# A prefetched expert block in the room of a smaller descriptor ring: one core, one layer step with 32 experts

## The chip, the cores and the metric

The kernel runs on one core of one Trainium2 chip. The metric is the device time of one execution in microseconds (us). Three executions of the kernel before took 1171.94, 1173.74 and 1175.29 us; the median is 1173.74 us. All data are 32-bit floats in HBM, and all weights are read once.

## What is computed

One layer of a diffusion backbone for 128 context tokens and 128 latent tokens, model width 1024. Cut to what matters here:

```
mod = silu(c) @ w_ada + b_ada                      # six vectors of 1024 for each token group
h   = rmsnorm(x) * g_mix * (1 + scale) + shift
z   = h @ w_in                                     # pool 512 | q | k | v 512 each | gates 2 x 1024
a   = pool_mixer(z.pool, w_pool) @ w_pa
o   = attention(q, k, v, cache_k, cache_v, rpb) @ w_pb
x   = x + gate_m * ((sigmoid(ga) * a + sigmoid(gb) * o) @ w_out)
h2  = rmsnorm(x) * g_ffn * (1 + scale_f) + shift_f
p   = softmax over the top 4 of 32 of (h2 @ w_router + b_router)
for e in range(32):                                # each expert reads 8 MB of w_up and 4 MB of w_down
    u = h2 @ w_up[e] + b_up[e]
    y = ((clip(u.up) + 1) * glu(u.gate)) @ w_down[e] + b_down[e]
    acc += p[:, e] * y
out = rmsnorm(x + gate_f * acc) * g_final
```

## The kernel before

**Stages.** The prologue, up to about 204 us, computes everything up to the merged branches: modulation, input projection, attention, pooling, branch projections. Then come the output projection (TensorE line L1475), the norm and the router. From 250 us on, the experts are worked through in 16 pairs. The tokens of a pair are gathered into two groups of 64 rows, so that two experts fill the 128 output rows of the matmuls. A pair has eight up blocks and four down blocks. A block is one DMA of 2,048 KB: for up, one k-block of 128 rows of both experts (or two k-blocks of one expert); for down, the same amount. The experts thus read 192 blocks.

**Order of the pairs.** TensorE does the up blocks of pair Q, then the down blocks of pair Q-1, then gathers the rows of pair Q+1. The first pair's up blocks (`up_first`) are followed at once by the second pair's (`up_second`), both on line L1555. After these, up blocks are on line L1615 and down blocks on L1630. The last down blocks are on L1650.

**Buffers.** `ring` is 16 slots of 8 KB a partition. The prologue's weights use single slots, the experts use pairs of slots, so that eight blocks fit. SyncE (SP) issues all weights in one fixed order. The function `put(n, at, ...)` waits until the semaphore `moe_free` has counted `at + 1` and then issues ring block n. Eight counts come from the prologue, the router stage and the output projection, as they give their slots free; after that TensorE adds one for each ring block that it has finished. So ring block n is issued when ring block n-8 is finished. One further block, the first pair's k-block 7, goes to `spare`, a place in the 13,056-column scratch tensor `arena`, and adds nothing to `moe_free`; SP issues it once the residual is done (`x2_ready`). That makes nine blocks which can be under way before TensorE has finished its first one.

**The prologue's order.** `MIX` lists the prologue's weight chunks in SP's order. The last ten are chunks of the input projection, two of `w_pa`, two of `w_pb` and four of `w_out`. Each waits on `pro_used` or `O_done` until its slot is free. GpSimd (POOL) issues the small loads on its own queue: `w_pool`, eight pieces of the relative position bias `rpb`, `cache_k`, `cache_v`, `g_ffn`, `w_router`, `b_router`. Then it waits for `bias_copied`, masks the bias in eight steps (L476, L479) and raises `bias_ready`. VectorE waits for that at L911, and the splits of the gate weights into two parts (L893, L896) that TensorE needs next (L1292 to L1294) stand behind it.

```
# POOL
part_load(kc, A_cache_k[0, 0].rearrange("h l d -> l h d"), L["kc"])
...
part_load(brt[:, :], A_b_router.to_broadcast([P, E]), L["brt"])
pool.wait_ge(bias_copied, 1)
```

Of the kernel before, what the change touches and what calls it, by code (L numbers as in the profile page):

```python
# [13 lines left out]
P = 128  # L14
# [28 lines left out]
PC = UPC + DNC  # L43
BC = BODY * PC
LAPS = BC // RING
FIRST_UP = UPC - 1
NC = PAIRS * PC - 1
LOOPS = (PAIRS - 4) // BODY
VEC = 44

# [22 lines left out]
def layer_kernel(nc, A_x_prompt, A_x_sample, A_cache_k, A_cache_v, A_c, A_c_ctx, A_w_ada, A_b_ada, A_g_mix,  # L73
# [13 lines left out]
    with ExitStack() as ctx:  # L87
# [15 lines left out]
        selbuf = sb("selbuf", [96, 2, CAP], BF16)  # L103
        ident = sb("ident", [P, P])
        iota = sb("iota", [P, CAP])
        iota_i = sb("iota_i", [P, CAP], I32)
        tab = sb("tab", [P, PAIRS + 1, 8])
        cur = sb("cur", [P, 8])
        small = sb("small", [P, 256])
        flags = sb("flags", [P, 4], I32)  # L110
        mhalf = sb("mhalf", [P, 1])
        pick = sb("pick", [P, 4])
# [81 lines left out]
        Af = in_slot(13, 0, 2, D)  # L194
        shf = in_slot(15, 0, 2, D)

        vecs = sb("vecs", [VEC, P])
        cT = sb("cT", [P, VEC])
        gffn = in_slot(9, 0, D)
        cs = in_slot(9, 1024, KB, 32)  # L200
        wpool = in_slot(9, 1280, 4, P)
# [1 line left out]
        cnt = region(6720, 4, PW)  # L203
        wrt = sb("wrt", [P, KB, E])
        brt = sb("brt", [P, E])
        selrow = sb("selrow", [P, 2, P])
        tri = sb("tri", [P, P])
        ones = sb("ones", [P, P])
        rt = sb("rt", [P, 2, 8, E])

        Am = small[:, 0:16].rearrange("p (g k) -> p g k", g=2)
# [39 lines left out]
        scat_done, acc_done, woT_done, woT_ready = sem("scat_done"), sem("acc_done"), sem("woT_done"), sem("woT_ready")  # L251
        hT_done, hTe_ready, y_ready = sem("hT_done"), sem("hTe_ready"), sem("y_ready")
        hT_split, unit_ready, unit_used = sem("hT_split"), sem("unit_ready"), sem("unit_used")
        yT_split, oT_top_ready, w_top_ready = sem("yT_split"), sem("oT_top_ready"), sem("w_top_ready")
        cur_ready, glu_ready = sem("cur_ready"), sem("glu_ready")
        fin_ss, fin_lo, fin_hi, last_scat, stored = (sem("fin_ss"), sem("fin_lo"), sem("fin_hi"), sem("last_scat"),
# [36 lines left out]
        @block.sync  # L293
        def _(sp):
            def mixing_chunk(c):
                s = ring[:, mix_slot[c], :]
                kind, m, k = MIX[c]
                if kind == "first":
                    return (s.rearrange("p (k s n) -> p k s n", k=2, s=2), w_first_v[:, 2 * k:2 * k + 2, :, m, :])
                if kind == "ada":  # L300
                    return s, w_ada_v[:, k, m * SLOT:(m + 1) * SLOT]
                if kind == "in":
                    return (s.rearrange("p (k n) -> p k n", k=4),
                            w_in_v[:, 4 * k:4 * k + 4, m * HALF:(m + 1) * HALF])
                w = {"pa": w_pa_v, "pb": w_pb_v, "out": w_out_v}[kind]
                return s.rearrange("p (k n) -> p k n", k=2), w[:, 2 * k:2 * k + 2, :]

            for row, src in ((0, A_c_ctx), (8, A_c[0]), (16, A_g_mix[0])):
                sp.dma_start(vecs[row:row + 8, :], src.rearrange("(k p) -> k p", p=P)).then_inc(L["vec"], 16)
            sp.dma_start(vecs[24:28, :], A_pool_scale[0].rearrange("(k p) -> k p", p=P)).then_inc(L["vec"], 16)  # L310
            sp.dma_start(vecs[28:44, :], A_b_ada[0][0:2 * D].rearrange("(k p) -> k p", p=P)).then_inc(L["vec"], 16)
            sp.dma_start(x[:, 0, :], A_x_prompt[0]).then_inc(L["x0"], 16)
            sp.dma_start(x[:, 1, :], A_x_sample[0]).then_inc(L["x1"], 16)
            for c in range(len(MIX)):
                if mix_before[c] is not None:
                    sp.wait_ge(pro_used, mix_before[c] + 1)
                elif mix_slot[c] >= RING0:
                    sp.wait_ge(O_done, 1)
                dst, src = mixing_chunk(c)
                if MIX[c][0] == "first":  # L320
                    for j in range(2):
                        sp.dma_start(dst[:, j], src[:, j]).then_inc(pro_loaded[mix_slot[c]], 16)
                else:
                    sp.dma_start(dst, src).then_inc(pro_loaded[mix_slot[c]], 16)

            def stream(r):

                def put(n, at, src, dst=None):
                    sp.wait_ge(moe_free, at + 1)
                    sp.dma_start(pair_slot(n) if dst is None else dst, src).then_inc(moe_loaded[n % RING], 16)  # L330

                def rows(e, c):
                    return w_up_v[e, :, c // 2, :] if c < UPC else w_down_v[e, :, (c - UPC) // 2, :]

                def halves(n):
                    return pair_slot(n).rearrange("p (a n) -> p a n", a=2)

                N = r * NC
                for kk in range(FIRST_UP):
                    if kk == FIRST_UP - 1:  # L340
                        if r == 0:
                            sp.wait_ge(x2_ready, 4)
                        else:
                            sp.wait_ge(y_ready, 2 * (1 + r * PAIRS))
                        sp.dma_start(spare, up_rows(0, KB - 1)).then_inc(spare_loaded, 16)
                    put(N + kk, N + kk, up_rows(0, kk), halves(N + kk))

                n0 = N + FIRST_UP
                for kk in range(KB):
                    put(n0 + kk, n0 + kk, up_rows(2, kk), halves(n0 + kk))  # L350
                for c in range(DNC):
                    put(n0 + UPC + c, n0 + UPC + c, rows(c % 2, UPC + c))

                with sp.Fori(0, LOOPS) as i:
                    N0 = N + FIRST_UP + PC
                    n0 = sp.snap(i * BC + N0)
                    e0 = sp.snap(i * (2 * BODY) + 2)
                    for h in range(BODY):
                        for c in range(PC):
                            m = h * PC + c  # L360
                            e = e0 + (2 * h + c % 2 + (2 if c < UPC else 0))
                            put(N0 + m, n0 + m, rows(e, c))

                n0 = N + FIRST_UP + PC + LOOPS * BC
                for c in range(PC):
                    put(n0 + c, n0 + c, rows(E - (4 if c < UPC else 6) + c % 2, c))
                n0 += PC
                for kk in range(KB):
                    put(n0 + kk, n0 + kk, up_rows(E - 2, kk), halves(n0 + kk))
                n0 += UPC  # L370
                for c in range(DNC):
                    put(n0 + c, n0 + c, down_rows(E - 4, 2 * c, 2 * c + 2), halves(n0 + c))
                n0 += DNC
                for c in range(DNC - 1):
                    put(n0 + c, n0 + c, down_rows(E - 2, 2 * c, 2 * c + 2), halves(n0 + c))
                dst = halves(n0 + 3)
                sp.wait_ge(moe_free, n0 + 4)
                sp.dma_start(dst[:, :, 0:D], down_rows(E - 2, 6, 7)).then_inc(tail_loaded, 16)
                sp.dma_start(dst[:, :, D:2 * D], down_rows(E - 2, 7, 8)).then_inc(moe_loaded[(n0 + 3) % RING], 16)

            def up_rows(e, kk):
                return A_w_up[0][e:e + 2].rearrange("e (c p j) n -> p c j e n", p=P, j=2)[:, kk // 2, kk % 2]

            def down_rows(e, j0, j1):
                v = A_w_down[0][e:e + 2].rearrange("e (c p j) n -> p c e j n", p=P, j=4)
                v = v[:, j0 // 4, :, j0 % 4:(j1 - 1) % 4 + 1]
                return v.rearrange("p e j n -> p e (j n)")

            stream(0)
            further_rounds(sp, read_flags(sp), stream)  # L390

            for t, y in enumerate((y_prompt, y_sample)):
                sp.wait_ge(fin_lo, t + 1)
                sp.wait_ge(fin_hi, t + 1)
                sp.dma_start(y[0], x[:, t, :]).then_inc(stored, 16)
            sp.wait_ge(stored, 32)
            sp.wait_ge(kv_stored, 32)
# [811 lines left out]
        def _(pe):  # L1209
# [19 lines left out]
            def keep_busy(n, bank):  # L1229

                for _ in range(n):
                    mm(ps[:, bank, 0:TOK], tri[:, :], selrow[:, :, :].rearrange("p a b -> p (a b)"), start=True, stop=True)

            def first_rows(hf, chunks):

# [323 lines left out]
            def up_first(R, chunk, second_half):  # L1559

                up_bias(R)
                for kk in range(KB):
                    if kk % 4 == 0:
                        pe.wait_ge(xg_ready, R * 2 + (kk // 4 + 1))
                    if kk == 2 and second_half is not None:
                        gather(R, 1, second_half)
                    if kk < FIRST_UP:
                        up_block(0, kk, both_experts(chunk(kk), 2 * FF)).then_inc(moe_free, 1)
                    else:
                        pe.wait_ge(spare_loaded, 16 * (R // PAIRS + 1))  # L1570
                        up_block(0, kk, [spare[:, a, :] for a in range(2)]).then_inc(first_used, 1)
# [189 lines left out]
```

## Time and profile before

| | |
|---|---|
| median of three executions | 1173.74 us (1171.94 to 1175.29) |
| profiled execution, first to last instruction | 1172.6 us |
| median less that span | 1.1 us |
| HBM read | 457.51 MB, 392 GB/s over the span |
| TensorE matmul busy | 1068.0 us (91%) |
| VectorE, ScalarE, POOL busy | 304.9, 141.2, 42.7 us |
| granted TensorE clock, mean | 0.982 |

The profile's times are us from the first instruction. A matmul of float32 operands shows as two records. A wait is named by the instruction that stood waiting and by what ended the wait; "SPq" is SyncE, whose instructions only issue DMAs. For the profiled execution no time apart from the span is given, so the span is what sums are made against.

### The profile page before, as it was taken

The page shows a single profiled execution, that of the slowest core. Times are in us where ns is not written, and L with a number is a line of the kernel's source. Part 1 is how long each engine was busy: PE and PEld are TensorE (multiplying, and loading weights), DVE is VectorE, ACT ScalarE, POOL GpSimd, SP SyncE. Part 2 cuts the span into 40 slices and gives each one's busy share as a digit, 9 for nine tenths or more (in the row PEclk, how much of TensorE's full clock was granted, in tenths as well). Part 3 has the DMA queues.
Part 4 walks back from the last instruction along what each step waited for, and adds up shares of the span by engine and source line. Part 5 has one row for each costly group of instructions (what it writes and reads, how often), then busy time and mean ns, then how long its engine had stood idle before and what let it go on. Part 6 is the DMA issues. An engine that isn't in the chain of part 4 may idle for free.

```text
span 1172.6 us, 13196 instructions
## 1 busy us (share of the span) xinstructions
PE 1068.0 (91%) x5399; PEld 505.0 (43%) x5399; DVE 304.9 (26%) x585; ACT 141.2 (12%) x275; POOL 42.7 (4%) x79
## 2 busy tenths in 40 slices
PE   7989999999999989898989897979898989797987
PEld 5755798454343424343434242424242424242422
DVE  3042767742212121212121212121212121212125
ACT  2013324111010101000001010101010101010111
POOL 3004000000000000000000000000000000000000
PEclk9999999999999999999999999999999999999999
DMA  9988464899999999999999999999999999999995
GB/s 333 407 325 259 169 258 139 339 421 422 429 418 429 428 426 429 429 428 429 428 429 428 429 429 428 428 428 429 428 429 429 428 429 429 428 429 422 421 421 215
DMA packets 51248, 459.64 MB, mean 392 GB/s; under 512 B 4444, under 2 KB 4504, under 8 KB 20648
## 3 DMA queue, kind: packets, MB, share of 16 engines
q1 hardware_dynamic: 49960, 455.12, 93.3%
q0 software_dynamic: 1024, 3.29, 1.1%
q10 hardware_dynamic: 224, 0.69, 0.2%
q8 instruction: 25, 0.41, 0.1%
q14 instruction: 15, 0.12, 0.0%
HBM read 457.51 MB, written 1.57 MB: 392 GB/s over the span
## 4 chain that ended last, share of the span: by engine, by line
PE 63%; DMA 31%; DVE 2%; issue 1%; SPq 1%; ACT 1%; POOL 0%; DVEq 0%; POOLq 0%; ACTq 0%
DMA ring<-in_w_down_dram 30%; PE ps L1615 17%; PE ps L1630 10%; PE ps L1555 6%; PE ps L1508 5%; PE ps L1519 5%; PE ps L1261 4%; PE ps L1475 2%; PE ps L1650 2%; PE ps L1277 1%; PE ps L1548 1%; PE ps L1535 1%; PE ps L1292 1%; PE ps L1294 1%; PE ps L1293 1%
## 5 line engine op out<-in xcount | busy, mean ns | idle before, releaser
L1615 PE MATMUL ps<-ring,arena 128*64 128x512 f32 x1664 | 364.5, 593 | 17.9 <-DMA ring<-in_w_up_dram 17.9
L1630 PE MATMUL ps<-ring,arena 128*64 128x512 f32 x896 | 209.1, 622 | 53.3 <-DMA ring<-in_w_down_dram 53.3
L1615 PEld LDWEIGHTS ps<-ring,arena 128*64 128x64 f32 x1664 | 121.0, 137 | 244.8 <-issue 242.5
L1630 PEld LDWEIGHTS ps<-ring,arena 128*64 128x64 f32 x896 | 72.5, 143 | 189.5 <-issue 170.5
L1115 DVE TENSOR_TENSOR arena<-ps,arena 128x512 f32<-128x512 f32 x64 | 44.2, 691 | 296.1 <-PE ps L1519 296.1
L1096 DVE TENSOR_SCALAR arena<-ps 128x512 f32<-128x512 f32 x32 | 20.6, 686 | 259.0 <-PE ps L1615 220.7
L1555 PE MATMUL ps<-ring,arena 128*64 128x512 f32 x368 | 80.8, 594 | 0.7 <-DVE arena L1098 0.7
L1508 PE MATMUL ps<-arena 128*128 128x128 f32 x512 | 63.6, 282 | 0.0
L1508 PEld LDWEIGHTS ps<-arena 128*128 128x128 f32 x512 | 61.7, 196 | 2.6 <-issue 2.4
L1519 PE MATMUL ps<-arena 128*128 128x512 f32 x128 | 57.8, 594 | 1.2 <-ACT arena L716 1.2
L1084 DVE TENSOR_SCALAR arena<-arena,cur 128x64 f32<-128x64 f32 x64 | 12.0, 249 | 162.7 <-PE ps L1527 160.2
L703 ACT ACTIVATE arena<-arena 128x512 f32<-128x512 f32 x32 | 19.5, 629 | 271.7 <-DVE arena L1096 271.7
L1555 PEld LDWEIGHTS ps<-ring,arena 128*64 128x64 f32 x368 | 26.2, 137 | 50.0 <-issue 48.4
L716 ACT ACTIVATE arena<-ps 128x512 f32<-128x512 f32 x30 | 16.3, 594 | 243.0 <-PE ps L1630 234.7
L1261 PE MATMUL ps<-ring 128*128 128x256 f32 x192 | 43.1, 384 | 0.0
L501 POOL COPY selbuf<-sel 96x128 bf16 (+1 forms) x16 | 11.2, 700 | 819.3 <-DVE arena L1098 811.1
L1261 PEld LDWEIGHTS ps<-ring 128*128 128x128 f32 x192 | 36.7, 193 | 7.1 <-issue 2.1
L1292 PE MATMUL ps<-parts 128*128 128x256 f32 x128 | 37.4, 292 | 1.9 <-DVE parts L896 1.9
L1294 PE MATMUL ps<-parts 128*128 128x256 f32 x128 | 36.9, 289 | 0.0
L1293 PE MATMUL ps<-parts 128*128 128x256 f32 x128 | 36.9, 288 | 0.0
L1106 DVE SCALAR_TENSOR_TENSOR arena<-arena 128x512 f32<-128x512 f32 x32 | 35.0, 1095 | 1.1
L1519 PEld LDWEIGHTS ps<-arena 128*128 128x128 f32 x128 | 23.1, 190 | 25.8 <-issue 23.8
(235 smaller groups left out, 802.4 us busy)
## 6 DMA issues: line engine op xcount, KB each, us to landing
ring<-in_w_up_dram SPq DMA_DIRECT2D x127, 2048.0 KB, 26.9
ring<-in_w_down_dram SPq DMA_DIRECT2D x63, 2048.0 KB, 23.2
ring<-in_w_in_dram SPq DMA_DIRECT2D x16, 1024.0 KB, 10.0
ring<-in_w_ada_dram SPq DMA_DIRECT2D x16, 1024.0 KB, 11.4
ring<-in_w_ada_dram SPq DMA_DIRECT2D x16, 512.0 KB, 11.7
ring<-in_w_out_dram SPq DMA_DIRECT2D x4, 1024.0 KB, 11.3
ring<-in_w_pa_dram SPq DMA_DIRECT2D x2, 1024.0 KB, 10.9
ring<-in_w_pb_dram SPq DMA_DIRECT2D x2, 1024.0 KB, 6.0
```

The costliest lines, as they stand in the source:

```text
L1106: V.scalar_tensor_tensor(out=gate[:, c].rearrange("q (j p) -> q j p", j=4), in0=hid[:, c].rearrange("q (p j) -> q j p", j=4), scalar=1.0, ...
L1115: V.tensor_tensor(acc[:, t, c], ps[:, SB + n, :], acc[:, t, c], ALU.add).then_inc(acc_done, 1)
L1261: ins = mm(ps[:, bank + b // 2, (b % 2) * TOK:(b % 2 + 1) * TOK], w[:, kk % 4, b * P:(b + 1) * P], hTm[:, kk, :], start=False, stop=(kk == ...
L1292: mm(out, w_top[:, n % 2, kk, :], hT_top[:, kk, :], start=(kk == 0), stop=False)
L1293: mm(out, w_top[:, n % 2, kk, :], hT_rest[:, kk, :], start=False, stop=False)
L1294: ins = mm(out, w_rest[:, n % 2, kk, :], hT_top[:, kk, :], start=False, stop=(kk == KB - 1))
L1475: ins = mm(ps[:, 2 * t + n, :], sgA[:, kk, t * P:(t + 1) * P], wo_[kk // 2][:, kk % 2, n * HALF:(n + 1) * HALF], start=(kk == 0), stop=(kk ...
L1508: ins = mm(ps[:, bank, (j % 4) * P:(j % 4 + 1) * P], h2[:, t, 2 * P * (j // 2) + j % 2:2 * P * (j // 2 + 1):2], oh[:, t, :], start=(t == 0 ...
L1519: mm(ps[:, SB + n, :], woT[:, t, :], yb[:, (n % 2) * HALF:(n % 2 + 1) * HALF], start=True, stop=True).then_inc(scat_done, 1)
L1555: ins = mm(ps[CAP * a:CAP * a + CAP, n, :], xgT[:, h, kk, CAP * a:CAP * a + CAP], w[a][:, n * HALF:(n + 1) * HALF], start=first, stop=(kk ...
L1615: ins = mm(ps[CAP * a:CAP * a + CAP, n, :], xgT[:, h, kk, CAP * a:CAP * a + CAP], w[a][:, n * HALF:(n + 1) * HALF], start=False, stop=(kk ...
L1630: ins = mm(ps[CAP * a:CAP * a + CAP, YB + n, :], hT[:, f, CAP * a:CAP * a + CAP], w[a][:, n * HALF:(n + 1) * HALF], start=(f == 0), stop=( ...
```

## The change

The descriptor ring of POOL's DMAs is set to 2,048 bytes a partition. `iota_i`, `cT`, `vecs` and `selrow` become places in `arena`, `small` is cut from 256 to 112 columns, and `tri` and `ones` become one tensor. The filler matmuls of `keep_busy` read `tri` and `ones` in place of `selrow`. A new tensor `early` of 4096 columns holds k-block 6 of the first pair. SP issues its load before the first chunk of `w_out`, with no wait. `FIRST_UP`, the number of the first pair's blocks that go through the ring, falls from 7 to 6, and the ring carries 190 blocks in place of 191. The load of `spare` comes behind all six. TensorE waits for `early_loaded` before k-block 6.

```diff
-FIRST_UP = UPC - 1
-NC = PAIRS * PC - 1
+FIRST_UP = UPC - 2
+NC = PAIRS * PC - 2
...
-        iota_i = sb("iota_i", [P, CAP], I32)
...
-        small = sb("small", [P, 256])
+        small = sb("small", [P, 112])
...
-        vecs = sb("vecs", [VEC, P])
-        cT = sb("cT", [P, VEC])
+        early = sb("early", [P, 2 * 2 * FF])
+        cT = region(11808, VEC)
+        vecs = arena[0:VEC, 11852:11852 + P]
+        iota_i = region(11984, CAP).bitcast(I32)
...
-        selrow = sb("selrow", [P, 2, P])
-        tri = sb("tri", [P, P])
-        ones = sb("ones", [P, P])
+        selrow = region(12800, 2, P)
+        masks = sb("masks", [P, 2, P])
+        tri, ones = masks[:, 0, :], masks[:, 1, :]
...
+            def load_early(r):
+
+                if r:
+                    sp.wait_ge(first_used, r)
+                sp.dma_start(early[:, :].rearrange("p (a n) -> p a n", a=2), up_rows(0, KB - 2)).then_inc(early_loaded, 16)
...
             for c in range(len(MIX)):
+                if c == AT["out", 0, 0]:
+                    load_early(0)
...
                 for kk in range(FIRST_UP):
-                    if kk == FIRST_UP - 1:
-                        if r == 0:
-                            sp.wait_ge(x2_ready, 4)
-                        else:
-                            sp.wait_ge(y_ready, 2 * (1 + r * PAIRS))
-                        sp.dma_start(spare, up_rows(0, KB - 1)).then_inc(spare_loaded, 16)
                     put(N + kk, N + kk, up_rows(0, kk), halves(N + kk))
+                if r == 0:
+                    sp.wait_ge(x2_ready, 4)
+                else:
+                    load_early(r)
+                    sp.wait_ge(y_ready, 2 * (1 + r * PAIRS))
+                sp.dma_start(spare, up_rows(0, KB - 1)).then_inc(spare_loaded, 16)
...
-                    mm(ps[:, bank, 0:TOK], tri[:, :], selrow[:, :, :].rearrange("p a b -> p (a b)"), start=True, stop=True)
+                    mm(ps[:, bank, 0:TOK], tri[:, :], masks[:, :, :].rearrange("p a b -> p (a b)"), start=True, stop=True)
...
                     if kk < FIRST_UP:
                         up_block(0, kk, both_experts(chunk(kk), 2 * FF)).then_inc(moe_free, 1)
+                    elif kk < KB - 1:
+                        pe.wait_ge(early_loaded, 16 * (R // PAIRS + 1))
+                        up_block(0, kk, both_experts(early[:, :], 2 * FF))
...
-    nc = _bacc.Bacc("TRN2", target_bir_lowering=False, num_devices=1)
+    nc = _bacc.Bacc("TRN2", target_bir_lowering=False, num_devices=1, dynamic_dma_scratch_size=2048)
```

## Rows read from the trace of the kernel before

**Rows 1.** The page, the span in 40 slices of 29.3 us.
```profile
GB/s 333 407 325 259 169 258 139 339 421 422 429 418 429 428 426 429 429 428 429 428 429 428 429 429 428 428 428 429 428 429 429 428 429 429 428 429 422 421 421 215
```

**Rows 2.** Waits on TensorE, 405 to 1137 us: total, times, longest.
```profile
PE ps L1630 <- DMA ring<-in_w_down_dram: 53.3, 24, 2.8
PE ps L1615 <- DMA ring<-in_w_up_dram: 17.9, 11, 2.0
```

**Rows 3.** Waits on TensorE, 250 to 405 us: the only one.
```profile
PE ps L1555 <- DVE arena L1098: 0.7, 1, 0.7
```

**Rows 4.** Chain that ended last, 340 to 411 us: start, length, what.
```profile
407.80 23.41 DMA ring<-in_w_down_dram
```

**Rows 5.** Windows: busy of each engine, clock, DMA share, GB/s.
```profile
166.00:168.00 2.00, 2.00 (x19) 2.00 (x18) 0.87 (x2) 0.00 (x0) 0.00 (x0) 1.00 0.00 0
...
350.00:352.00 2.00, 2.00 (x12) 0.42 (x7) 0.00 (x0) 0.00 (x0) 0.00 (x0) 1.00 0.82 279
...
411.00:1137.00 726.00, 651.85 (x3102) 261.72 (x3098) 128.87 (x242) 60.75 (x112) 9.11 (x12) 0.98 1.01 428
```

**Rows 6.** Timeline of SyncE: start, length, line, DMA, count.
```profile
157.74 0.89 SPq L324 DMA_DIRECT2D ring<-in_w_pb_dram  x2
170.62 6.27 SPq L324 DMA_DIRECT2D ring<-in_w_out_dram  x4
...
286.38 14.88 SPq L330 DMA_DIRECT2D ring<-in_w_down_dram  x4
...
348.92 8.29 SPq L330 DMA_DIRECT2D ring<-in_w_down_dram  x4
```

**Rows 7.** Waits on SyncE, 250 to 410 us.
```profile
SPq L330 <- PE ps L1615: 53.6, 6, 15.0
```

**Rows 8.** DMAs issued at 229.83, 286.38, 333.40, 348.92: us to landing.
```profile
ring<-in_w_up_dram SPq DMA_DIRECT2D x1, 2048.0 KB, 7.1
...
ring<-in_w_down_dram SPq DMA_DIRECT2D x1, 2048.0 KB, 11.4
...
ring<-in_w_up_dram SPq DMA_DIRECT2D x1, 2048.0 KB, 18.2
...
ring<-in_w_down_dram SPq DMA_DIRECT2D x1, 2048.0 KB, 7.7
```

**Rows 9.** Timeline of POOL, 86 to 111 us.
```profile
87.74 1.01 POOL L403 DMA_DIRECT2D ring<-in_w_pool_dram  x1 [75.61 <-DMA ring<-in_w_in_dram]
88.74 4.89 POOL L403 DMA_DIRECT2D ring<-in_rpb_dram  x8
...
94.52 0.89 POOL L403 DMA_DIRECT2D ring<-in_cache_v_dram  x1
...
96.84 0.56 POOL L403 DMA_DIRECT2D brt<-in_b_router_dram  x1
110.60 1.11 POOL L476 TENSOR_SCALAR_AFFINE_SELECT ring<-ring 64x384 f32<-64x384 f32 x1 [13.20 <-ACT ring L587]
```

**Rows 10.** The page's DMA issues on POOL's queue: median us to landing.
```profile
out_dram<-ring POOLq DMA_DIRECT2D x1, 256.0 KB, 3.2
...
ring<-in_w_pool_dram POOLq DMA_DIRECT2D x1, 256.0 KB, 7.6
...
ring<-in_rpb_dram POOLq DMA_DIRECT2D x8, 64.0 KB, 9.1
```

**Rows 11.** Waits on VectorE, 105 to 125, and on TensorE, 86 to 206.
```profile
DVE ring L911 <- POOLq L483: 4.1, 1, 4.1
...
PE ps L1292 <- DVE parts L896: 1.9, 1, 1.9
```

**Rows 12.** Window behind that wait of TensorE, columns as in rows 5.
```profile
120.00:124.00 4.00, 3.96 (x20) 3.96 (x21) 3.30 (x6) 0.00 (x0) 0.00 (x0) 0.57 0.00 0
```

**Rows 13.** Timeline of TensorE: bias flip and output projection.
```profile
107.44 1.95 PE L1355 MATMUL ps<-ring 128*128 128x512 f32 x4 [1.42 <-DVE arena L828]
...
204.65 22.56 PE L1475 MATMUL ps<-ring,arena 128*128 128x512 f32 x52 [0.41 <-PE ps L1439]
```

More of the change, by code:

```diff
@@ L253, in layer_kernel @@
         hT_split, unit_ready, unit_used = sem("hT_split"), sem("unit_ready"), sem("unit_used")
+        early_loaded = sem("early_loaded")
         yT_split, oT_top_ready, w_top_ready = sem("yT_split"), sem("oT_top_ready"), sem("w_top_ready")
@@ L313, in _, with up_rows @@
             sp.dma_start(x[:, 1, :], A_x_sample[0]).then_inc(L["x1"], 16)
+            def load_early(r):
+                if r:
+                    sp.wait_ge(first_used, r)
+                sp.dma_start(early[:, :].rearrange("p (a n) -> p a n", a=2), up_rows(0, KB - 2)).then_inc(early_loaded, 16)
+            def up_rows(e, kk):
+                return A_w_up[0][e:e + 2].rearrange("e (c p j) n -> p c j e n", p=P, j=2)[:, kk // 2, kk % 2]
             for c in range(len(MIX)):
+                if c == AT["out", 0, 0]:
+                    load_early(0)
                 if mix_before[c] is not None:
@@ L379, in stream @@
                 sp.dma_start(dst[:, :, D:2 * D], down_rows(E - 2, 7, 8)).then_inc(moe_loaded[(n0 + 3) % RING], 16)
-            def up_rows(e, kk):
-                return A_w_up[0][e:e + 2].rearrange("e (c p j) n -> p c j e n", p=P, j=2)[:, kk // 2, kk % 2]
             def down_rows(e, j0, j1):
```

## Prediction

> **What bounds the kernel now.** I read the rates of the page's slices first [rows 1]. From the ninth slice on, the weight stream runs at 418 to 429 GB/s but for the last slice; before that there are holes, down to 139 GB/s. So a load that is moved into a hole should take its time off the stream behind it. That holds only where the stream sets the pace, so the next view is the waits of TensorE by stage. Between 405 and 1137 us TensorE waits for weights again and again, 71.2 us in all [rows 2]. Between 250 and 405 us it waits for no weights at all, and for only 0.7 us of anything [rows 3]. The chain of work that ended last says the same: it enters the weight stream for good with the block issued at 407.80 us [rows 4]. Before that the chain lies on TensorE. The reader is to see two stages. Up to about 405 us TensorE is behind, and the stream must wait for it. After that the stream is behind, and the end of the program is the end of the stream plus a fixed tail.
>
> The pace of the stream is one block of 2,097,152 bytes at 428 GB/s [rows 5], which is 4.90 us. This is the most that one block loaded ahead can bring.
>
> **The early load itself.** It is one issue on SP and one block. SP has issued `w_pb` by 157.74 + 0.89 = 158.63 us and then waits until 170.62 us for a slot [rows 6]. The new issue needs no slot, so it goes out at about 158.7 us. The two pieces of `w_pb` (2 MB) are before it in the queue, and between 166 and 168 us nothing at all is moved [rows 5]. Its 4.90 us fit ahead of 170.62 us, so `w_out`, which TensorE needs at 204.65 us [rows 13], isn't delayed. Cost 0; if the hole were gone, `w_out` would land 4.9 us later, and with it the whole of the 34 us until then would have to be used up before that cost anything.
>
> **What follows for the stream.** Number the blocks in the order in which TensorE uses them: P0 to P7 are the first pair's up blocks, P8 to P15 the second pair's, P16 to P19 the first pair's down blocks, P20 to P27 the third pair's up blocks, P28 the next down block. Before, ring block n is P(n+1) for n of 7 and more, and it needs ring block n-8 finished, that is P(n-7). So P(j) needs P(j-8). After, ring block n is P(n+2) for n of 6 and more and needs P(n-6). Again P(j) needs P(j-8). With `early` and `spare` emptied once and not used again, the one block more of room exists only at the start. From P16 on, the earliest moment at which a block may be issued is the same as before, and it is set by TensorE.
>
> Now the slack. On an empty queue a block lands 7.1 us after its issue (up, issued at 229.83) [rows 8]. P16 is issued at 286.38 us [rows 6] and lands after 11.4 us [rows 8], so it stands about 11.4 - 7.7 = 3.7 us behind others. With the stream 4.9 us ahead that slack is gone, the queue runs dry for about 1.2 us, and 3.7 us of the lead are left. P28 is issued at 348.92 us [rows 6], after SP has waited 15.0 us for TensorE's L1615 [rows 7]. It lands after 7.7 us [rows 8], at 356.6 us. The block before it was issued at 333.40 and landed 18.2 us later, at 351.6 us [rows 8]; one block of streaming behind that is 356.5 us. So P28 found the queue just empty already in the kernel before. In the window from 350 to 352 us the rate falls to 279 GB/s [rows 5], a loss of 2 x (1 - 279/428) = 0.7 us. In the changed kernel the blocks before P28 land up to 3.7 us sooner, the queue waits for TensorE, and P28 starts at the same moment. The lead of 4.9 us has become idle time of the DMA engines before 350 us. Gain: 0 us by the landings, at most 0.7 us if all of that dip goes. I take 0.
>
> TensorE itself gets no earlier start: it has no wait for weights in that stage [rows 3], its eight blocks of the first pair are the same matmuls, and the filler matmuls read other data of the same shape. Those edits, the smaller `small` and the moved tables cost nothing: no instruction is added on VectorE, ScalarE or POOL. The wait for `early_loaded` is met 100 us before. The `spare` load keeps its place in time, as it waited for `x2_ready` behind the same six blocks.
>
> **The smaller descriptor ring.** This is the part that can cost. POOL issues 14 loads from 87.74 to 97.40 us (96.84 + 0.56) [rows 9]. The first lands only after 7.6 us, at 95.3 us, and the bias pieces after 9.1 us in the median [rows 10]. So by the time anything has landed nearly all are under way, and POOL was never held. The next work of POOL is the masking at 110.60 us [rows 9]: 13.2 us of room. Behind it stands VectorE's L911, which waited 4.1 us for it, and behind that the splits, for which TensorE waited 1.9 us [rows 11]. So whatever delays the masking past 110.60 us goes into the time one for one, because all up to 405 us hangs on TensorE.
>
> The loads aren't alike in pieces: `cache_k`, `cache_v` and `w_router` are 1024 contiguous runs each (128 partitions by 8), `w_pool` 512, each of the eight bias pieces 256, the other two 128 each. That is 5,888 runs, of which 4,608 (all up to `cache_v`, whose issue begins at 94.52 us) go out with nothing landed [rows 9]. The old ring thus took at least 4,608 runs, and one of an eighth of its bytes is sure to take 576 only. How much more it takes, and whether POOL stands still until a whole older load has landed, no row shows. From below: if room comes free as single runs are moved, POOL's last issue slips by less than the 13.2 us, cost 0. From above: `cache_k` must wait for about the fifth bias piece, issued at 88.74 + 4 x 4.89/8 = 91.2 us [rows 9], which lands 9.1 us later or some more, near 101 us; `cache_v` must wait for `cache_k`, and `w_router` for `cache_v`. A load of 256 KB takes 3.2 us on a quiet queue and 7.6 us beside the weights [rows 10]. The last issue then ends at 101 + 2 x 3.2 + 1.5 = 108.9 us to 101 + 2 x 7.6 + 1.5 = 117.7 us, where 1.5 us is the issue of the last two loads. Against 110.60 us this is 0 to 7.1 us. SyncE's loads are nearly done by then, so I lean to the quiet row, and take 1 us for the likeliest case, with 3 us as its upper end. The bias pieces must land before TensorE's L1355 at 107.44 us [rows 13]; the last can be issued near 97 us and lands near 106 us, so they still come in time.
>
> A longer idle of TensorE has a second price. After its 1.9 us of waiting the granted clock is 0.57 over 120 to 124 us, most of it at the lower of the two levels, 1.2 GHz [rows 12]. About 1.7 us are lost there already (4 us x 0.43). If the idle time grows to 5 us or more, I allow 1 us more.
>
> **The sum.** Span 1172.6 us; early load 0; lead of the stream 0 (bounds -0.7 and -4.9); POOL's ring +1 (bounds 0 and +8 with the clock): 1173.6 us of span. The median of the runs stands 1.1 us above the profiled span, so 1174.7 us.
>
> **Rivals.** (a) The lead is kept: the stream stays one block ahead to the end and the time falls by 4.9 us, to 1168.8 us. For it: the holes before the ninth slice [rows 1], and 71 us of waits for weights later [rows 2]. Against it: P28's landing 7.7 us after its issue and SP's wait of 15.0 us for TensorE. It would need TensorE to finish P20 at least 4.9 us earlier. (b) The ring stalls POOL and the masking slips by 4 to 8 us: 1178 to 1182 us. For it: the chain through L911 has no slack. Against it: 13.2 us of room and few weights in the queues after 100 us. It decides once POOL's last issue ends later than 114 us. The Trainium skill, "Debugging Trainium Hangs", section 4, Descriptor Overflow, speaks for this direction: it gives POOL's descriptors a finite room of 16 KiB a partition and names too many of them as a cause of hangs. (c) The early load gets in the way of others on the shared engines. It runs from about 165 to 170 us, where between 166 and 168 us nothing else is moved [rows 5], so I give it nothing of its own.
>
> **How the numbers follow.** A run of this kernel tells a change from none at about 0.3%, 3.5 us. No lead and a stall of 0 to 3 us: 0.65, time 1173 to 1177. Rival (b): 0.23. Rival (a): 0.08. The remaining 0.04 is for effects of placement I can't see, to either side. Faster by over 0.3%: 0.10; within: 0.65; slower: 0.25. The range must hold 8 in 10. It takes the likeliest case, half of (b) and the near side of (a): 1170.5 to 1180.0 us.
>
> **What would show it.** In the profile after, the early block is issued near 158.7 us. P16 is issued near 286.4 us and P28 near 348.9 us, both plus the delay of the masking, and both land 7 to 8 us after their issue; the DMA rate dips in some windows between 286 and 350 us where it did not before. TensorE's first wait for weights comes as long after its first up block as before. POOL's last load issue ends before 111 us, or the masking starts as much later as the whole program ends later. I'm wrong if P28 is issued, relative to TensorE's start on the experts at 250 us, earlier than before, or if the time falls by more than 3.5 us.

## The result

The changed kernel takes 1180.26 us in the median of four executions (1177.73 to 1181.25), the kernel before 1172.84 us over four (1171.5 to 1175.29). The ratio is 1.0058 with a 95% interval of 1.0046 to 1.0070: slower by 7 us. The forecast was 1174.7 us in a range of 1170.5 to 1180.0 us; the median lies 0.3 us above that range. The profiled execution took 1181.18 us for a span of 1179.4 us, 6.8 us more than the span of the kernel before.

The rates of the page's slices, beside [rows 1]. The stream is slower than before in the ninth to eleventh slice (391, 402 and 392 GB/s in place of 421, 422 and 429) and in the thirteenth (401 in place of 429):

```profile
GB/s 333 408 302 269 165 286 171 307 391 402 392 430 401 428 428 427 428 430 429 428 427 428 429 429 429 427 428 429 429 430 427 428 429 430 430 427 424 420 421 215
```

Timeline of POOL, columns as in [rows 9]:

```profile
89.44 1.01 POOL L413 DMA_DIRECT2D ring<-in_w_pool_dram  x1 [77.29 <-DMA ring<-in_w_in_dram]
90.44 3.07 POOL L413 DMA_DIRECT2D ring<-in_rpb_dram  x5
97.26 1.24 POOL L413 DMA_DIRECT2D ring<-in_rpb_dram  x2 [3.75 <-issue]
104.79 0.62 POOL L413 DMA_DIRECT2D ring<-in_rpb_dram  x1 [6.29 <-issue]
105.40 0.90 POOL L413 DMA_DIRECT2D ring<-in_cache_k_dram  x1
112.36 0.90 POOL L413 DMA_DIRECT2D ring<-in_cache_v_dram  x1 [6.06 <-issue]
113.25 0.56 POOL L413 DMA_DIRECT2D ring<-in_g_ffn_dram  x1
116.35 0.90 POOL L413 DMA_DIRECT2D wrt<-in_w_router_dram  x1 [2.54 <-issue]
117.24 0.56 POOL L413 DMA_DIRECT2D brt<-in_b_router_dram  x1
117.81 0.58 POOL L486 TENSOR_SCALAR_AFFINE_SELECT ring<-ring 64x384 f32<-64x384 f32 x1
```

POOL stands still four times, 3.75 + 6.29 + 6.06 + 2.54 = 18.6 us. The profile puts these waits down to "issue", as there is no semaphore of the program behind them. Each stop ends 0.3 to 0.4 us after a whole load has landed: `w_pool` at 96.95 us, the seventh bias piece at 104.40, `cache_k` at 112.02, `cache_v` at 116.04. The masking starts the moment the last load is out, at 117.81 us in place of 110.60. Who waits for it, on VectorE (105 to 135 us) and on TensorE (86 to 130 us), beside [rows 11]:

```profile
DVE ring L921 <- POOLq L493: 7.9, 1, 7.9
```

```profile
PE ps L1302 <- DVE parts L906: 5.3, 1, 5.3
...
PE ps L1365 <- DMA ring<-in_rpb_dram: 2.6, 1, 2.6
```

TensorE waits 5.3 us for the split weights in place of 1.9, and 2.6 us for the late bias piece. From here on the whole program is late by one amount: the expert stage's first up matmul starts at 256.85 us in place of 250.01.

SyncE's timeline, columns as in [rows 6]:

```profile
165.51 0.47 SPq L320 DMA_DIRECT2D early<-in_w_up_dram  x1
177.46 6.31 SPq L337 DMA_DIRECT2D ring<-in_w_out_dram  x4
...
293.21 14.88 SPq L343 DMA_DIRECT2D ring<-in_w_down_dram  x4
...
355.75 8.29 SPq L343 DMA_DIRECT2D ring<-in_w_down_dram  x4
```

P16 goes out at 293.21 and P28 at 355.75, both 6.83 us later than in [rows 6], neither a moment sooner against TensorE. What they took to land, each in a query of its own, beside [rows 8]:

```profile
ring<-in_w_down_dram SPq DMA_DIRECT2D x1, 2048.0 KB, 7.5
...
ring<-in_w_down_dram SPq DMA_DIRECT2D x1, 2048.0 KB, 7.6
```

P16 took 11.4 us before. Now both meet an empty queue. Two windows, columns as in [rows 5]:

```profile
286.00:296.00 10.00, 9.27 (x51) 4.61 (x48) 5.92 (x7) 3.03 (x4) 0.29 (x1) 1.00 0.90 340
...
411.00:1137.00 726.00, 655.23 (x3108) 265.02 (x3106) 130.00 (x248) 59.68 (x110) 9.12 (x12) 0.98 1.01 428
```

A first part of the lead is spent here: around 290 us the DMA engines are idle for a time (340 GB/s). The long stage behind runs at 428 GB/s as before.

The records of issue and landing show where the rest goes. Counted from the first up matmul of the experts, so that what happened in the prologue drops out (us, issue and landing):

| block | before | changed |
|---|---|---|
| P16 | 36.4, 47.7 | 36.4, 43.9 |
| P18 | 46.3, 57.5 | 46.3, 55.3 |
| P27 | 83.4, 101.6 | 83.4, 100.6 |
| P28 | 98.9, 106.6 | 98.9, 106.6 |
| P30 | 106.3, 117.4 | 106.3, 117.7 |
| end of the span | 922.6 | 922.5 |

Every issue from P16 to P30 is at the same place. The lead of the landings is 3.8 us at P16, 2.2 us at P18, 1.0 us at P27 and gone at P28. TensorE's first wait for weights begins 170.8 us after its first up block in both.

### The profile page after: what moved, and what is told of

It is laid out like the page before. It is cut to its first block, busy times and chain, and to the rows that moved or that the text cites. A ratio compares the mean times of both kernels' runs of the same rounds, so it can differ in the third digit from the quotient of the medians.

```text
span 1179.4 us, 13214 instructions
## 1 busy us (share of the span) xinstructions
PE 1072.1 (91%) x5399; PEld 508.9 (43%) x5399; DVE 305.4 (26%) x585; ACT 141.3 (12%) x275; POOL 42.2 (4%) x79
## 3 DMA queue, kind: packets, MB, share of 16 engines
q0 software_dynamic: 1024, 3.29, 1.0%
## 4 chain that ended last, share of the span: by engine, by line
PE 61%; DMA 31%; issue 3%; DVE 2%; POOL 1%; SPq 1%; ACT 1%; DVEq 0%; POOLq 0%; ACTq 0%
DMA ring<-in_w_down_dram 30%; PE ps L1628 17%; PE ps L1643 10%; PE ps L1565 6%; PE ps L1518 5%; PE ps L1529 5%; PE ps L1271 4%; PE ps L1485 2%; PE ps L1663 2%; PE ps L1558 1%; PE ps L1545 1%; PE ps L1302 1%; PE ps L1304 1%; PE ps L1303 1%; PE ps L1235 1%
## 5 line engine op out<-in xcount | busy, mean ns | idle before, releaser
L1565 PEld LDWEIGHTS ps<-ring,arena 128*64 128x64 f32 x352 | 25.0, 137 | 47.7 <-issue 46.1
```

What stands on the lines that cost most here:

```text
L1565: ins = mm(ps[CAP * a:CAP * a + CAP, n, :], xgT[:, h, kk, CAP * a:CAP * a + CAP], w[a][:, n * HALF:(n + 1) * HALF], start=first, stop=(kk ...
```

## The experiments

Each run was timed beside the kernel before; ratios are to that kernel and given with their 95% intervals. Changes are against the kernel named.

**The ring alone.** Against the kernel before:

```diff
-    nc = _bacc.Bacc("TRN2", target_bir_lowering=False, num_devices=1)
+    nc = _bacc.Bacc("TRN2", target_bir_lowering=False, num_devices=1, dynamic_dma_scratch_size=2048)
```

> The kernel before with the ring of 2,048 bytes and nothing else. Theory A (the whole loss is POOL standing still for room in the ring): POOL's last load is issued near 117.2 us in place of 96.8, the masking starts near 117.8 in place of 110.6, and the time is 6 to 7.5 us over the kernel before (ratio 1.005 to 1.006). Theory B (placement of the small tensors, or the early load in the way of others, makes the loss): within 1.5 us of the kernel before.

Measured: 1178.76 us, ratio 1.0049 (1.0037 to 1.0061). POOL's timeline:

```profile
101.76 0.62 POOL L403 DMA_DIRECT2D ring<-in_rpb_dram  x1 [6.20 <-issue]
...
109.73 0.90 POOL L403 DMA_DIRECT2D ring<-in_cache_v_dram  x1 [6.46 <-issue]
...
115.28 0.58 POOL L476 TENSOR_SCALAR_AFFINE_SELECT ring<-ring 64x384 f32<-64x384 f32 x1
```

The stops are at the same four places, and the time is 5.7 us over the kernel before by the ratio, just under the 6 to 7.5 us expected. The masking starts at 115.28 us and not near 117.8, but POOL began at 86.29 us in this execution: from the first load to the masking it is 29.0 us, in the changed kernel 28.4, before 22.9 [rows 9]. So one argument of the builder makes the slowdown, and no placement or early load is needed for it. The 1 us between this and the changed kernel is within the two intervals.

**The loads on another queue, with and without the early block.** Against the changed kernel, and the same against the kernel before:

```diff
 # POOL
-            pool.wait_ge(pro_loaded[mix_slot[c_after]], 16 * mix_held[c_after])
-            part_load(wpool, ...)          # and the 13 loads behind it
 # ScalarE, behind z_out(2)
+            act.wait_ge(pro_loaded[mix_slot[c_after]], 16 * mix_held[c_after])
+            act_load(wpool, ...)           # the same 14 loads in the same order
             act.wait_ge(pool_done, 1)
```

> The changed kernel, with POOL's 14 prologue loads issued by ScalarE, which makes no use of the small ring. Theory A with P(j) needs P(j-8): no stall, the early block is loaded, and the time is that of the kernel before to within 1 us, with P28 landing 7 to 8 us after its issue. Theory C (the lead is kept, the stall only hid it): 4.9 us under the kernel before, 1168 us. Theory B: still 5 us or more over the kernel before.

> Control: the kernel before, large ring, with the same 14 loads issued by ScalarE. Theory A: within 1 us of the kernel before and within 1 us of the run with the early block. Theory C: 4 to 5 us slower than the run with the early block.

Measured: 1172.73 us, ratio 0.9999 (0.9989 to 1.0009) with the early block, 1173.58 us, ratio 0.9999 (0.9990 to 1.0008) without. The loss is gone, and no gain is behind it. P16 again met an empty queue, landing 7.5 us after its issue, and P28 after 7.8 us. This settles it against the rival that the lead is kept. The first of the two has the moved tensors, the early load and the ring of 2,048 bytes of the changed kernel, so none of these shows a cost once POOL's 14 loads no longer go through the ring.

**A semaphore for each bias piece.** In the changed kernel the eighth piece went out at 104.79 us. The first had landed at 98.42 and the seventh at 104.40. All eight raise one semaphore. Against the changed kernel:

```diff
-                        part_load(dst, src, L["rpb"])
+                        part_load(dst, src, rpb_sems[4 * r + 2 * kr + par])
...
-            pe.wait_ge(L["rpb"], 16 * 8)
+            for s in rpb_sems:
+                pe.wait_ge(s, 16)
```

> The changed kernel with a semaphore of its own for each of the eight bias pieces. In the changed kernel the eighth piece was issued at 104.79, right after the seventh had landed, though the first had landed at 98.4. If POOL waits by the shared semaphore's count, the eighth now goes out near 98.8 us, cache_k near 102 or later, the masking starts 3 to 5 us sooner than 117.8 and the time falls by as much, to about 1176. If POOL waits for room in the order of issue whatever the semaphore, nothing changes: 1180.

Measured: 1176.66 us, ratio 1.0036 (1.0019 to 1.0053), 2.6 us better than the changed kernel by the ratios. But the two intervals overlap and the nine executions spread from 1175.33 to 1182.78 us, so the gain in time is likely and not shown; the trace shows what POOL does. Its timeline:

```profile
86.54 1.01 POOL L414 DMA_DIRECT2D ring<-in_w_pool_dram  x1 [74.41 <-DMA ring<-in_w_in_dram]
87.54 3.08 POOL L414 DMA_DIRECT2D ring<-in_rpb_dram  x5
94.65 1.99 POOL L414 DMA_DIRECT2D ring<-in_rpb_dram  x3 [4.03 <-issue]
100.11 0.90 POOL L414 DMA_DIRECT2D ring<-in_cache_k_dram  x1 [3.47 <-issue]
105.26 0.90 POOL L414 DMA_DIRECT2D ring<-in_cache_v_dram  x1 [4.25 <-issue]
...
111.02 0.90 POOL L414 DMA_DIRECT2D wrt<-in_w_router_dram  x1 [4.19 <-issue]
```

The eighth piece goes out with the other two, at 96.02 us, 0.3 us after the first had landed (95.71). `cache_k` goes 0.4 us after the landing of the fifth piece (99.75). From first load to masking it is now 25.9 us (112.48 - 86.54), 2.4 us less. So it matters whether the loads that POOL waits for share a semaphore. With one each it waits for the landing of single pieces; with one for all it waited for the seventh.

**A ring of 4,096 bytes.** Against the kernel before, as in the first run, with 4096.

> The kernel before with a ring of 4,096 bytes and nothing else. 
Measured: 1173.50 us, ratio 1.0002 (0.9993 to 1.0011). POOL's timeline:

```profile
88.82 4.91 POOL L403 DMA_DIRECT2D ring<-in_rpb_dram  x8
93.73 0.90 POOL L403 DMA_DIRECT2D ring<-in_cache_k_dram  x1
103.58 0.90 POOL L403 DMA_DIRECT2D ring<-in_cache_v_dram  x1 [8.95 <-issue]
...
105.92 0.56 POOL L403 DMA_DIRECT2D brt<-in_b_router_dram  x1
109.64 0.58 POOL L476 TENSOR_SCALAR_AFFINE_SELECT ring<-ring 64x384 f32<-64x384 f32 x1 [3.15 <-ACT ring L587]
```

One stop of 8.95 us, which ends 0.4 us after the eighth bias piece has landed (103.14 us). It costs nothing: the last load is out at 106.48 us, and the masking waits for ScalarE as before. Here a stall of POOL is free up to the point where ScalarE brings it its input.

**Less work on TensorE ahead of P8.** This is to see whether a free slot is all that the lead lacks. Both kernels have the loads on ScalarE. They leave out three quarters of the up product of k-blocks 1 to 3 of the first pair:

```diff
-            def up_block(h, kk, w, first=False):
-                for n in range(4):
+            def up_block(h, kk, w, first=False, groups=range(4)):
+                for n in groups:
...
-                        up_block(0, kk, both_experts(chunk(kk), 2 * FF)).then_inc(moe_free, 1)
+                        up_block(0, kk, both_experts(chunk(kk), 2 * FF),
+                                 groups=range(3, 4) if kk in (1, 2, 3) else range(4)).then_inc(moe_free, 1)
```

> The kernel before with the loads on ScalarE, and k-blocks 1 to 3 of the first pair multiply one of their four column groups in place of all four, so that part of the first pair's up product is left out. That takes 3 x 0.75 x 3.44 = 7.7 us from TensorE ahead of P8. Theory A (with the ring full the stream waits for TensorE up to P28, and just meets it there without the early block): the stream was running without a break already, so the time falls by at most 1 us, to 1172.5 to 1173.5. Rival (TensorE alone sets the pace up to P28): it falls by all of 7.7 us, to 1166.

> The changed kernel with the loads on ScalarE and the same matmuls of the first pair left out. Theory A: now the slots come free soon enough, the queue never runs dry, and the block loaded ahead is worth its 4 to 4.9 us: 4 us or more under the run without the early block. If the early block is worth nothing for another reason, the two are the same to within 1 us.

Measured: without the early block 1173.35 us, ratio 0.9999 (0.9990 to 1.0008); with it 1169.26 us, ratio 0.9961 (0.9947 to 0.9974). So 7.7 us less work on TensorE are worth nothing alone, and the early block is worth nothing alone, but both together are worth 4.1 us. From the first up matmul P16 is issued at 28.6 us in both, and P28 lands at 106.9 us without and at 101.7 us with the early block, 5.1 us sooner, and 4.9 us of it are left at the end of the span. Windows of the run with the early block, where the changed kernel with the loads on ScalarE and all its work had 370 and 419 GB/s:

```profile
280.00:300.00 20.00, 20.00 (x100) 8.62 (x97) 2.61 (x4) 1.68 (x3) 0.00 (x0) 1.00 1.02 428
300.00:345.00 45.00, 45.00 (x221) 17.99 (x219) 11.76 (x23) 4.87 (x9) 0.69 (x1) 1.00 1.01 428
```

**The same with all work done, first try.** TensorE's scatter of the rows of pair Q-1 is moved behind the slots that it held up. Against the changed kernel with the loads on ScalarE:

```diff
                         gather(Q + 1, b, GB + b)
-                    scatter(Q)
...
 # up and up_last
                 for kk in range(KB):
+                    if kk == 2:
+                        scatter(Q - 1)
                     if kk == 3:
                         turn_weights(Q - 1)
```

In the second pair the gather went from kk == 2 to 3, the hidden rows' transposes from 3 to 4 and the bias matmuls from 2 to 6.

> A try at a faster kernel, all work done: the changed kernel, loads on ScalarE, TensorE's scatter of the finished rows moved from the end of a pair to behind the second k-block of the next pair's up blocks, and in the second pair the gather one block later and the bias matmuls four blocks later. P20 comes free about 3.6 us sooner. Theory A: P28 is issued near 345.3 us by the clock of the kernel before and lands near 353, and the time falls by 2.5 to 3.6 us, to about 1170.5. If the stream isn't what holds, no change.

> Control: the kernel before with the same reordering on TensorE and the loads on ScalarE, no early block. Theory A: the stream has no lead to keep, so the time is within 1 us of the kernel before.

Measured: 1173.18 us, ratio 1.0000 (0.9990 to 1.0011), and without the early block 1173.42 us, ratio 1.0002 (0.9994 to 1.0011). A miss for the first. P28 was issued at 96.4 us from the first up matmul and landed at 105.4, 1.3 us sooner than before. But the scatter now stood between P21 and P22, so P30 was issued at 107.6 in place of 106.3. It landed at 118.8 in place of 117.4. The later issue alone doesn't explain that: in the control P30 was issued at 107.6 too and landed at 116.7. With the early block the stream ran at 270 GB/s from 358 to 360 us, though P30 had been issued at 357.1 us, and no run shows what slowed it:

```profile
358.00:360.00 2.00, 2.00 (x12) 0.72 (x10) 0.00 (x0) 0.00 (x0) 0.00 (x0) 1.00 0.86 270
```

TensorE also waited 1.6 us for ScalarE's copies of gathered rows, in both kernels, as the scatter no longer stood between the gather and the matmuls that wait for them:

```profile
PE ps L1561 <- ACT arena L705: 1.6, 2, 0.9
```

The early block's lead over the control was 1.2 us at P28 and had turned into 2.0 us of lag at P30, so this pair of runs doesn't tell whether the lead could have been kept.

**Second try.** Against the same kernel. The scatter goes behind kk == 6 and the weights' transposes to 7; in the second pair the gather stays at 2, the bias matmuls go to 5 and the scatter to 6.

```diff
-                    if kk == 3:
-                        turn_weights(Q - 1)
+                    if kk == 6:
+                        scatter(Q - 1)
+                    if kk == 7:
+                        turn_weights(Q - 1)
```

> The changed kernel with the loads on ScalarE and, on TensorE, the scatter moved behind the sixth k-block of the next pair (the try before had it behind the second, where P28 landed 1.3 us sooner but P30 then came 1.3 us later), the gather of the second pair left in its place, its bias matmuls behind five blocks. Theory A: P28 is issued near 95.3 us after the first up matmul of the experts in place of 98.9, P30 near 102.7 in place of 106.28, and P30 lands 2.3 to 3.5 us sooner than the kernel before's 117.4; the time falls by that, to 1170 to 1171.3. If nothing between P20 and P28 matters to the end, 1173.5.

> Control: the kernel before with the same order on TensorE and the loads on ScalarE, no early block. Theory A: the stream has no lead, only the dip at P30 of about 1 us goes: 1172.5 to 1173.5. Rival (the order on TensorE alone brings the gain): as fast as the run with the early block.

Measured: with the early block 1171.51 us, ratio 0.9984 (0.9976 to 0.9993); without it 1173.94 us, ratio 1.0000 (0.9987 to 1.0012). This is the only version here that beats both kernels with all work done, by 1.9 us over the one before and 2.4 us over its control. From the first up matmul P28 is issued at 96.4 us, P30 at 103.3, and P30 lands at 115.8 against 117.4 before and 116.5 without the early block. The span ends 920.9 us after the first up matmul in place of 922.6, and 923.0 without the early block. The gain is a little under the 2.3 to 3.5 us expected. P28 came at 96.4 and not at 95.3, but it took 9.6 us to land and so didn't find the queue empty. The lead over the control was 2.7 us at P23 and 0.65 us from P24 on: P24 landed 7.0 us after P23 in place of 4.9, though 10.5 us after its own issue, with 322 GB/s from 326 to 329 us:

```profile
326.00:329.00 3.00, 3.00 (x18) 1.01 (x16) 0.00 (x0) 0.00 (x0) 0.00 (x0) 1.00 0.94 322
```

The control has P30 landed 0.9 us sooner than the kernel before and doesn't end sooner, as its P46 landed 6.4 us after P45 in place of 4.9, though 23 us after its own issue. So of the 2.1 us between the two profiled spans only 0.65 stand at P30, and the other 1.5 come at P46 of the control. No run shows what made the stream slow at P24 and at P46. That the version with the early block is faster is shown by the times; that its gain is the early block's lead, kept past P30, is shown for 0.65 us only.

## Why the prediction was right or wrong

**The early block is worth nothing: right, by its own steps.** P(j) needs P(j-8) in both kernels, SP's issues stand at the same places against TensorE, the queue runs dry at P16, and P28 meets an empty queue. The 3.7 us of lead foretold behind P16 were 3.8. Between P16 and P27 more of it went than I had worked out, as P18 and P19 also came late (6.6 and 5.5 us behind the block before, in place of 4.9); it didn't matter, since P28 takes all. That the lead is lost to TensorE's pace in freeing slots is shown by the runs with part of the up product left out: there it stays at 5.1 us from P16 to P28.

**The early load's own cost: right.** It went out behind `w_pb` and `w_out` was issued as late as before against its own slots. It was issued at 165.51 us, that is 158.7 plus the delay. The window that I gave it, ending before `w_out`, was just long enough: it landed at 177.10, `w_out` went out at 177.46. The program is 6.8 us late ahead of it, where TensorE starts on the split weights (126.89 us in place of 120.04), and 6.8 us late behind it.

**POOL's ring: the direction was seen, the size was not.** The step that failed is the term "POOL's ring +1" of the sum. It measured 6.2 us: of the 6.8 us by which the expert stage is late, 0.65 us were there before TensorE's L1358 (104.78 us against 104.13). The rest is TensorE's wait for the masking, which began 7.2 us later. The case behind the bound of 0, room that comes free as single runs are moved, is refuted: POOL stood still until whole loads had landed. Three steps of the likeliest case failed.

- The start. `cache_k` could not go at 101 us but at 105.40, because the eighth bias piece had to wait until the seventh of a shared semaphore had landed. So the last bias piece was issued at 104.79 and landed at 109.23 us, where I had 97 and 106, and TensorE's L1365 did wait for it.
- The quiet row. SyncE's loads were not done: `cache_k` took 6.6 us beside a load of `w_in` that took 6.4. Only `cache_v` (3.7 us), `w_router` and `b_router` (3.1 us each) came near 3.2 us.
- The row itself. The 3.2 us of [rows 10] are those of `out_dram<-ring`, a store of 256 KB, and I used them for loads.

The last issue ended at 117.80 us, next to the upper bound of 117.7. That is luck: the start was 4.4 us later than in that sum, and the two loads together took 4.9 us less than its two times 7.6. That the median came out only 0.3 us above the range is no merit of the sum either, since its likeliest value is 5.6 us too low and "within 0.3%", at 0.65, did not happen. Rival (b), with 4 to 8 us and a chance of 0.23, is what happened, with its deciding point: the last issue ended later than 114 us.

**The clock's price: wrong.** I allowed 1 us for a longer idle of TensorE ahead of the split weights. It waited 5.3 us and not 1.9, and the 4 us behind it had a granted clock of 0.59, against 0.57 before [rows 12]:

```profile
127.00:131.00 4.00, 4.00 (x22) 4.00 (x22) 3.14 (x6) 0.00 (x0) 0.00 (x0) 0.59 0.00 0
```

The longer wait had the same low-clock stretch behind it, so nothing was added there. A new one came elsewhere, behind the 2.6 us of waiting for the late bias piece, where the granted clock had been 1.00 before, after a wait of 1.4 us (107.40 to 109.30 us):

```profile
109.28 3.29 PE L1365 MATMUL ps<-ring 128*128 128x512 f32 x4 [2.61 <-DMA ring<-in_rpb_dram]
```

```profile
109.20:112.50 3.30, 3.22 (x4) 0.96 (x5) 2.71 (x6) 0.00 (x0) 0.14 (x1) 0.59 0.57 195
```

These matmuls took 3.29 us in place of 1.95 [rows 13], and the next 16 (L1332) 1.49 in place of 1.16. The 1.7 us didn't reach the total: TensorE only came later to its wait for the split weights, and POOL's masking decides when that ends.

## What to carry to other kernels

Before a load is moved ahead, write down for each later block which event frees its buffer. If a stage in between is paced by the consumer with the same number of buffers, the lead can be handed back there, however bandwidth-bound the rest is. Here it paid only together with an earlier release of the buffers. A smaller descriptor ring is a change of the program and not only of the memory map: count the contiguous runs of each load of that queue against it, and see what the queue's engine has to do next.

## What was not expected of the hardware

POOL waited for ring room by whole landed loads: each of the four stops ended 0.3 to 0.4 us after such a landing. With eight loads on one semaphore the eighth waited until the seventh had landed (104.40 us, issue at 104.79), though the first had been there for 6 us; with a semaphore for each, it went 0.3 us after the first. The run with 4,096 bytes agrees: by the count above, `w_pool` (landed at 95.37 us) and the first bias piece (96.57) would have made room for `cache_v`, and POOL stood until the eighth piece had landed (103.14, issue at 103.58). The stop shows in the profile as idle time with the releaser "issue". Only sharing among the eight bias pieces was tried; whether the wait is for the last issued of those on a semaphore or for a count that can't be told apart stays open.
